# RWKV core of a twelve-part model on one core: chunk parity on partition halves, whole 128x128 transposes

## The reference

```python
def step(state, inp):
    r_t, w_t, k_t, v_t, kk_t, a_t = inp
    sa = jnp.einsum('bhvk,bhk->bhv', state, kk_t)
    state = (state * w_t[:, :, None, :]
             - sa[..., None] * (kk_t * a_t)[:, :, None, :]
             + v_t[..., None] * k_t[:, :, None, :])
    return state, jnp.einsum('bhvk,bhk->bhv', state, r_t)
s0 = jnp.zeros((B, N_HEADS, HEAD_DIM, HEAD_DIM), f32)
_, y = lax.scan(step, s0, (tmaj(rh), tmaj(wh), tmaj(kh), tmaj(vh), tmaj(kk), tmaj(ah)))
```

## Time and profile before

| | |
|---|---|
| median of 3 runs | 2310.64 us (2310.57 to 2314.3) |
| span of the profiled execution | 2303.6 us |
| PE, PEld busy | 2176.2 (94%), 2079.3 (90%) us, 23136 instructions each |
| VectorE (DVE), ScalarE (ACT) busy | 1552.0 (67%), 1204.9 (52%) us |
| mean granted TensorE clock | 0.988 |

### The profile page before, as it was taken

One profiled execution on the slowest core, in us unless ns is written; L12 is line 12 of the kernel. 1 busy time (PEld: TensorE's weight loads), 2 busy tenths in 40 slices (PEclk: granted clock), 3 DMA queues, 4 the chain that ended last, 5 costly groups with the idle time before them and its releaser, 6 DMA issues. The chain is left out here.

```text
span 2303.6 us, 55968 instructions
## 1 busy us (share of the span) xinstructions
PE 2176.2 (94%) x23136; PEld 2079.3 (90%) x23136; DVE 1552.0 (67%) x2405; ACT 1204.9 (52%) x2058; POOL 36.1 (2%) x51
## 2 busy tenths in 40 slices
PE   6887899999999999999989888999999999999998
PEld 6777799999999988899988778999998999898998
DVE  7763465566665688665588735655777777876776
ACT  5733454455544456554458435544676444776443
POOL 0000000000000011000000000000100000100000
PEclk9899999999999999999989999999999999999999
DMA  5310355543455433355533103555333554434553
GB/s 204 128 48 4 110 176 181 180 140 120 153 194 183 163 112 124 123 192 191 183 101 123 54 4 111 192 191 182 129 115 133 193 190 155 147 120 147 182 191 110
DMA packets 88436, 327.16 MB, mean 142 GB/s; under 512 B 9808, under 2 KB 9936, under 8 KB 87632
## 3 DMA queue, kind: packets, MB, share of 16 engines
q1 hardware_dynamic: 87984, 322.66, 41.3%
q0 software_dynamic: 288, 2.10, 0.3%
HBM read 323.67 MB, written 1.05 MB: 141 GB/s over the span
## 5 line engine op out<-in xcount | busy, mean ns | idle before, releaser
L2184 PE MATMUL bank<-h_split,w_split 128*128 128x256 f32 x3176 | 912.7, 287 | 14.3 <-DVE h_split L2403 8.6
L2185 PE MATMUL bank<-h_split,w_split 128*128 128x256 f32 x3176 | 898.1, 283 | 0.0
L2186 PE MATMUL bank<-h_split,w_split 128*128 128x256 f32 x3176 | 897.6, 283 | 0.0
L2372 DVE TENSOR_TENSOR w_split<-ring_a,w_split 128x1024 fp32r<-128x1024 f32 x474 | 568.0, 1224 | 196.9 <-ACT w_split L2269 195.4
L2184 PEld LDWEIGHTS bank<-h_split,w_split 128*128 128x128 f32 x3176 | 602.9, 190 | 26.3 <-DVE h_split L2403 11.3
L2185 PEld LDWEIGHTS bank<-h_split,w_split 128*128 128x128 f32 x3176 | 598.6, 188 | 1.4
L2186 PEld LDWEIGHTS bank<-h_split,w_split 128*128 128x128 f32 x3176 | 597.8, 188 | 0.0
L2269 ACT ACTIVATE w_split<-ring_a 128x1024 fp32r<-128x1024 f32 x474 | 483.4, 1049 | 44.1 <-PE bank L664 23.7
L2206 PE MATMUL bank<-act_split,d_split 128*128 128x256 f32 x1008 | 285.4, 283 | 3.8 <-DVE act_last L2464 2.4
L2207 PE MATMUL bank<-act_split,d_split 128*128 128x256 f32 x1008 | 285.2, 283 | 0.0
L2208 PE MATMUL bank<-act_split,d_split 128*128 128x256 f32 x1008 | 285.1, 283 | 0.0
(11 more groups left out here) (302 smaller groups left out, 3256.4 us busy)
## 6 DMA issues: line engine op xcount, KB each, us to landing
ring_a<-wa SPq DMA_DIRECT2D x474, 512.0 KB, 3.7
ring_d<-wd SPq DMA_DIRECT2D x132, 512.0 KB, 4.3
tab_sb<-tab SPq DMA_DIRECT2D x1, 2384.0 KB, 13.2
hT<-na POOLq DMA_DIRECT2D x2, 1024.0 KB, 5.1
xT<-x SPq DMA_DIRECT2D x1, 1024.0 KB, 4.8
out<-xT SPq DMA_DIRECT2D x1, 1024.0 KB, 3.9
vec_sb<-vec SPq DMA_DIRECT2D x1, 288.0 KB, 4.8
tab_sb<-tab SPq DMA_DIRECT2D x1, 65.0 KB, 4.6
```

What stands on the lines that cost most here:

```text
L2184: mm(dst, w[:, 0, ks], x[:, 0, k, :], start=(k == 0), stop=False)
L2185: mm(dst, w[:, 0, ks], x[:, 1, k, :], start=False, stop=False)
L2186: last = mm(dst, w[:, 1, ks], x[:, 0, k, :], start=False, stop=(k == KT - 1))
L2372: v.tensor_tensor(w_split[:, u % 4, 1, :], ring_a[:, u % 4, :], w_split[:, u % 4, 0, :].bitcast(f32), ALU.subtract).then_inc(s["w_lo"], 1)
```

## The change

Chunk parity, not head parity, is now on partition halves of what the levels hold: partitions 0 to 63 are the even chunk of a pair, 64 to 127 the odd one, and the columns of a head pair n are the two heads side by side. So X of a pair and head pair is a 128x128 block, and its transpose is one `nc.tensor.transpose`. XT and Q have heads on the halves.

- `to_tokens` makes eight 128x128 transposes per call. `level_turned` and `turned_zero` make eight in two groups of four, each into a bank of its own (2 and 3).
- The levels use four banks: product and update both 0 and 1, turned blocks 2 and 3. Scores are in pairs of the banks 4 to 7.
- Both banks of the updated inverse are copied by ScalarE (`copy_x`), into every other 64 columns.
- `mask` works on two banks at a time; for the first pair the key columns of scores 0 and 1 are masked before the query columns. `level0t` goes; the first turned matrix of both chunks comes from TensorE.
- `solve` writes two banks, of which ScalarE copies one (`copy_u`) and VectorE the other (`u_other`), 64 partitions each; u lies where Q was, so the waits of `copy_u` for y and state go.
- `parted` is used 8 times a layer. `gain` and the copies of v_first move before the levels on ScalarE, `gated` behind the first pair's levels on VectorE; `bonus_sum` and `score_part` are spread over the levels.

```diff
-        B = [ctx.enter_context(nc.psum_tensor(f"bank{i}", [P, 512], f32)) for i in range(8)]
+        banks = ctx.enter_context(nc.psum_tensor("banks", [P, 8, 512], f32))
+        B = [banks[:, i, :] for i in range(8)]
...
             def to_tokens(i):
-                b0, b1 = eight(B[i % 4][:, :]), eight(B[i % 4 + 1][:, :])
-                for n, h in each_head():
-                    even = mm(b0[h, n, :], block(i % CHN), ident_of(h), start=True, stop=True)
-                    odd = mm(b1[other(h), n, :], block(i % CHN + 1), ident_of(h), start=True, stop=True)
-                even.then_inc(s["tok_mm"], 1)
-                odd.then_inc(s["tok_mm"], 1)
+                t = slice(P * (i % 4 // 2), P * (i % 4 // 2) + P)
+                for n in range(KT):
+                    block = (qkv[:, 16 + n, t], qkv[:, 8 + n, t], oT[:, n, t])[i // 4]
+                    last = nc.tensor.transpose(B[i % 4 + n // 4][:, P * (n % 4):P * (n % 4) + P], block, T("ident"))
+                    if n % 4 == 3:
+                        last.then_inc(s["tok_mm"], 1)
...
+            def turn_blocks(a, g):
+                for n in range(4 * g, 4 * g + 4):
+                    last = nc.tensor.transpose(turned_bank(g)[:, P * (n % 4):P * (n % 4) + P],
+                                               X_[a // 2][:, P * n:P * n + P], T("ident"))
+                last.then_inc(s[f"xt_mm{g}"], 1)
...
-            def level_turned(a, lv):
-                for n, h in each_head():
-                    even = mm(b0[h, n, :], Xc[a][h, n, :], ident_of(h), start=True, stop=True)
-                    odd = mm(b1[other(h), n, :], Xc[a + 1][h, n, :], ident_of(h), start=True, stop=True)
+            def level_turned(a, lv, g):
+                q = 2 * r + a // 2
+                pe.wait_ge(s["xn_ready"], 8 * q + 2 * lv)
+                pe.wait_ge(s[f"xtn_ready{g}"], 6 * q + lv)
+                turn_blocks(a, g)
...
             def level_product(a, lv):
+                for n, e, t, h, half in blocks():
+                    last = mm(level_bank(t)[h, n, :], scb[a // 2][half, e, n, CH:2 * CH], X_of(a // 2, half, n, e),
+                              start=True, stop=True)
...
             def level_update(a, lv):
+                for n, e, t, h, half in blocks():
+                    last = mm(level_bank(e)[half, n, :], XT_of(a // 2, h, n, t), Q_of(a // 2, h, n, t),
+                              start=True, stop=True)
...
                 if c and second:
-                    if c % 2:
-                        parted(c if c == 1 else 4)
+                    parted((1, 4, 7)[c - 1])
...
-            for i in range(4):
-                score_part(0, i)
-            level_zero(0)
-            level_zero(1)
+            score_part(0, 0)
+            score_part(0, 1)
+            level_zero(0, 0)
+            level_zero(0, 1)
+            score_part(0, 2)
             level_product(0, 1)
-            bonus_sum(0)
-            turned_zero(1)
-            bonus_sum(1)
+            turned_zero(0, 0)
+            turned_zero(0, 1)
+            score_part(0, 3)
...
-            def copy_x(c, lv):
-                q, t = 2 * r + c // 2, c % 2
-                act.wait_ge(s[f"xn_mm{t}"], 4 * q + lv)
-                A(Xc[c], eight(level_bank(c, 1)[:, :]), ACT.Copy).then_inc(s[f"xn_ready{t}"], 1)
+            def copy_x(a, lv):
+                act.wait_ge(s["xn_mm"], 4 * (2 * r + a // 2) + lv)
+                for e in range(2):
+                    A(X_half(a, e), level_bank(e), ACT.Copy).then_inc(s["xn_ready"], 1)
...
             def copy_u(c):
                 act.wait_ge(s["u_mm"], 4 * r + c + 1)
-                if c:
-                    act.wait_ge(s["y_mm"], 5 * r + c)
-                    act.wait_ge(s["st_mm"], 3 * r + c)
-                A(u_, eight(chain_bank(c, "r")[:, :]), ACT.Copy, scale=-1.0).then_inc(s["u_ready"], 1)
+                A(u_[c // 2][half_of(c), 0, :, :], u_banks()[half_of(c), 0, :, :], ACT.Copy, scale=-1.0)\
+                    .then_inc(s["u_ready"], 1)
...
+            def u_other(c):
+                dve.wait_ge(s["u_mm"], 4 * r + c + 1)
+                v.tensor_scalar(u_[c // 2][half_of(c), 1, :, :], u_banks()[half_of(c), 1, :, :], -1.0, None, ALU.mult)\
+                    .then_inc(s["u_side"], 1)
```

More of the change, by code:

```diff
@@ L494, in turned_zero @@
[L494 to L519, removed]
@@ L521, in level_update @@
-            def level_update(a, lv):
[L523 to L533, removed]
-                    even = mm(b0[h, n, :], XTc[a][h, n, :], Qc[a][h, n, :], start=True, stop=True)
-                    odd = mm(b1[h, n, :], XTc[a + 1][o, n, :], Qc[a + 1][o, n, :], start=True, stop=True)
-                even.then_inc(s["xn_mm0"], 1)
-                odd.then_inc(s["xn_mm1"], 1)
@@ L551, in last_turned @@
-            def last_turned(c):
-                q, t = counts(c)
-                pe.wait_ge(s[f"q_ready{t}"], 6 * q + 6)
-                pe.wait_ge(s[f"xtn_ready{t}"], (5 + t) * q + 4 + t)
-                b = eight(level_bank(c, 2)[:, :])
-                for n, h in each_head():
-                    last = mm(b[h, n, :], Qc[c][h, n, :], XTc[c][h, n, :], start=True, stop=True)
-                last.then_inc(s[f"xt_mm{t}"], 1)
+                if a and i == 3:
+                    pe.wait_ge(s["bonus_ready"], 4 * r + 4)
+                elif a or i > 1:
+                    pe.wait_ge(s["score_ready"], 10 * r + (5, 7, 8)[i] if a else 10 * r + i + 1)
@@ new lines, in score_part @@
+                b = score_banks(a, i)
+                for m in range(4 * (i % 2), 4 * (i % 2) + 4):
+                    for e in range(2):
+                        h = slice(HD * e, HD * e + HD)
+                        for c in (a, a + 1):
+                            left = qkv[h, 8 + m, tok(c)] if i >= 2 else oT[h, m, tok(c)]
+                            last = mm(b[half_of(c), e, m % 4, :], left, qkv[h, m:m + 25:24, tok(c)],
+                                      start=True, stop=True)
+                last.then_inc(s["score_mm"], 1)
@@ new lines, in blocks, with level_zero @@
+            def blocks(first=0, count=KT):
+                for n in range(first, first + count):
+                    for e in range(2):
+                        for t in range(2):
+                            yield n, e, t, slice(HD * e, HD * e + HD), slice(HD * t, HD * t + HD)
+            def level_zero(a, e):
+                pe.wait_ge(s["lt_ready"], 4 * r + a + e + 1)
+                if a:
+                    pe.wait_ge(s["q_ready"], 12 * (2 * r + 1))
+                for n in range(KT):
+                    for half in (slice(0, HD), slice(HD, P)):
+                        last = mm(level_bank(e)[half, n, :], scb[a // 2][half, e, n, CH:2 * CH], ident_of(half),
+                                  start=True, stop=True)
+                last.then_inc(s["lz_mm"], 1)
@@ new lines, in unit_lower, with factor_zero @@
+            def unit_lower(a, e):
+                dve.wait_ge(s["score_ready"], 10 * r + (8 if a else 2))
+                lt = scb[a // 2][:, e, :, CH:2 * CH]
+                v.tensor_tensor(lt, lt, wide("eye", KT), ALU.add).then_inc(s["lt_ready"], 1)
+            def factor_zero(a):
+                for e in range(2):
+                    dve.wait_ge(s["lz_mm"], 4 * r + a + e + 1)
+                    v.tensor_tensor(X_half(a, e), level_bank(e), wide("level0", KT), ALU.mult)                        .then_inc(s["q_ready"], 1)
@@ new lines, in factor @@
+            def factor(a, lv):
+                dve.wait_ge(s["lx_mm"], 5 * (2 * r + a // 2) + lv)
+                for t in range(2):
+                    v.tensor_tensor(eight(stream(Q_[a // 2], t)), level_bank(t), wide(f"level{lv}", KT), ALU.mult)                        .then_inc(s["q_ready"], 1)
+            def u_other(c):
+                dve.wait_ge(s["u_mm"], 4 * r + c + 1)
+                v.tensor_scalar(u_[c // 2][half_of(c), 1, :, :], u_banks()[half_of(c), 1, :, :], -1.0, None, ALU.mult)\
+                    .then_inc(s["u_side"], 1)
```

392 lines of the change are left out of this document (205 added, 187 removed).

## The result

| | before | after |
|---|---|---|
| median of 4 runs each | 2310.61 us (2309.42 to 2314.3) | 2270.72 us (2269.39 to 2273.41) |
| span of the profiled execution | 2303.6 us | 2268.4 us |
| PE, PEld busy | 2176.2, 2079.3 us, 23136 instructions each | 2167.8, 2071.8 us, 21472 each |
| clock | 0.988 | 0.990 |

The ratio is 0.9827, interval 0.9812 to 0.9842: 39.9 us less, where 27.6 was forecast; 2283.0 was predicted, and the result lies inside the range of 2261 to 2305, on its low side. 1,664 records went, as counted, but TensorE's busy time fell by only 8.4 us: what went is idle time between records.

The account below looks back on a forecast made before the run. No engine was saturated; round trips and TensorE's stops for instructions filled the two RWKV cores' gaps. Terms -3.5 - 6.2 - 12.5 - 9 + 1.2 + 2.4 = -27.6 us gave span 2276, median 2283; range 2261 to 2305.

Parts of the forecast that it names:

- A: Token transposes at the start of each RWKV core: shorter by 2.1 and 1.4 us in the two layers, -3.5.
- B: First score to first level update: key halves masked first, update at t+10.0 against 12.88 and 13.33, -6.2 us.
- C: Four levels of the first chunk pair: 5.7 us a level including 0.3 for stops, 22.8 a layer, -12.5.
- D: Second pair's levels woven with the state chain: gaps of 9 to 10 halved, 43 us a layer, -9.
- E, waits and switches: Chain's tail to first output unit, plus costs: self-waits +1.2 us, switches between 64x64 and 128x128 shapes +2.4.
- the supply rival: Both cores: instruction supply is the whole bound, 4.3 us per packet, -56 us, 2255; chance of more than -38: 0.12.
- Latency only: Both cores: stops stay at other places, or VectorE's mask holds the levels; about -8 us, 2303; chance 0.2.
- The clock falls: Clock falls in the token transposes and stays low through the first pair's levels; +20 us, 2331; chance 0.1.

Follow-up runs that it names:

- The second run: Changed kernel with v, kb and bb turned to tokens again by 64x64 f32 matmuls instead of whole transposes; 2279.78 us, ratio 0.9874.
- both edits: Changed kernel with both X and the tokens turned again by 64x64 f32 matmuls, all 1,664 records back; 2305.58 us, ratio 0.9990.
- the dummies: Changed kernel plus one-column 64x64 matmuls behind each level update: 16 or 32 in the first pair, 16 in the second; 2275.86, 2287.23, 2277.50 us.
- the wide matmul: Changed kernel with old state carried into new by one 128x512 f32 matmul instead of 16 of 64x64; 2275.38 us, with split inverse copy 2274.45.
- the burst: Changed kernel plus 640 one-column dummy matmuls behind the first level update of a layer; 2407.46 us, ratio 1.0434.

## Why the prediction was right, and where it was off

**A**, forecast -3.5, measured -4.0, with stage A at 7.2 for 7.5. The sum's order of events held. The second run confirms that the stops were the cost: the 64x64 form puts A at 10.0.

**B**, forecast -6.2, measured -7.4, stages 9.42 for 10.0. I gave all of it to the masks' order, and most of it does come with the new order: B had no stop for issue before, and with the turning's records back it still gains 6.6. With the tokens' records back as well it gains 4.1. Of the 3.2 that go, 0.8 is the 64x64 turning by itself and 1.0 a stop in the scores at 158.91; the rest was not separated from a clock of 0.88 in that stage of layer 1.

**C**, forecast -12.5, measured -13.2; a level 5.37 for 5.4, without the 0.3 for stops. The working added up product, turning and copies as if the path had set the 6.37 of before. For levels without a stop that holds (6.38 at 160.36, 5.74 with the old turning in the new layout). But the stops of C were 6.6 us before and none now, and with the turning's records back C is 28.51 and 26.67. So half of the gain is stops, which the working took as gone without a reason. That was close, and luck in part: a level issues 172 records, not 150, and at the usual 3.9 per 127 they need 5.3 of its 5.37. Layer 1's 5.2 more in C, at a clock of 0.89, are in the gain too; the clock need not be their cause, since with both edits C sums to 58.2 at 1.00, for 58.1 before.

**D**, forecast -9, measured -13.4. This is the step that failed in size: "Gaps of 9 to 10 remain; with a fifth of the records gone I halve them: 43". The gaps nearly vanished, 1.6 and 1.0 of idle PE. The windows of before had said how much was to be had: 7.5 and 6.3 of idle PE, of which 12.4 together were stops. Now stops are 0.9, and busy PE is 2.2 less. The trace of before also had the better price: stops in D end 3.98 and 3.88 apart, at 199.31, 203.29 and 207.17:

```profile
199.31 0.21 PE L517 MATMUL bank<-planes 64*64 64x64 f32 x1 [0.32 <-issue]
...
203.29 0.51 PE L641 MATMUL bank<-work,hT 64*64 64x64 f32 x10 [0.51 <-issue]
...
207.17 0.21 PE L515 MATMUL bank<-planes 64*64 64x64 f32 x1 [0.54 <-issue]
```

1,565 records at 3.9 per 127 are 48.1, the stage as measured (layer 2: 47.6 for 46.81). I took 3.40 instead, the shortest of all intervals, and so saw supply as a set of stops on top of a path, where in D it was the pace. At 3.9 the 1,304 records left need 40.0; the stage took 41.0 and 40.5. That is also all but TensorE's own busy time, 39.4. No stop for issue is left in D of layer 2, and 0.9 in layer 1, so by the trace D now stands on TensorE's own work; whether slow delivery also stretches busy stretches is open: the dummies could not tell, and the wide matmul brought a wait of its own.

**E, waits and switches**, forecast +3.6 in all, not located; measured +2.4, all in E. A wait of a solve for the turned copy, 0.8 in each layer and none before, is 1.6 of it; the rest was not traced further. The 1.2 for self-waits is of the right size (0.20 each, four of one line are 0.8; the line of the earlier trace rows is the state part of y, not of the right side); switches between shapes are nowhere visible as a cost: the eight transposes follow the last 64x64 record of the product at once.

**The span and the median.** I set the median 7.0 above the profiled span. All runs listed with a span lie 2.0 to 2.1 above it; the profiled execution of before was simply 4.9 below the median. So 12.3 us of error are 7.6 of the sum (35.2 for 27.6) and 4.7 of this. The 39.9 lie outside the band of the forecast itself (-15 to -38) and in that of the supply rival, which had a chance of 0.12; the result is inside the range only because the range took in part of that rival. By the spans, 35.2, the forecast's band holds.

**The rivals.** *Supply is the whole bound* gave 2255 from 4.3 us a packet and all 13.1 packets gone. Its mechanism is nearer to the truth than I allowed: with the records back 37.6 of 39.9 are gone. But it is not the whole: of the 35.2 between the spans 20.8 are stops, and the 7.4 of B had none. Its price was too high, because 4.3 is the mean over cores in which B and E wait for other things; measured with all that the 64x64 form brings, a packet is worth 2.9 (37.6 / 13.1), 3.7 in the turning (28.9 for 992 records, 7.8 packets), 2.1 in the tokens (10.9 for 5.3). *Latency only* is refuted: by it the stops would have stayed at other places, but of 22.5 us 1.7 are left. *The clock falls* is refuted for this kernel: A to D kept 1.00, stage A with transposes alone included. The Trainium skill (TensorE: Matmul & The Clock Gate, "Part 4: PE-mode transpose") says that transposes do not count as busy for the clock in the way matmuls do; by that rule A was where it would fall, and this trace does not bear it out. Before, and in the kernels with the records back, the clock fell in one or two stages (C 0.89 and 0.94, B 0.88). It was 0.97 in E of layer 2 even in the changed kernel, and 0.91 in E of layer 1 in the kernel with the tokens' records back.

## What to carry to other kernels

Count instructions, not array time, where small f32 matmuls stand in a row: each 64x64 one is two records and two weight loads, and where TensorE stopped for them, the ends of stops in a row were mostly 3.4 to 4.0 us apart. Divide a stage's records by 127 and its time by that; where the result is near what D took with its stops (3.7 to 3.9) and "issue" ends the stops, supply is the pace, and wider instructions help even if the array's work is the same. The quotient alone does not tell: D of the changed kernel has 3.9 to 4.0 with hardly a stop. The packets' own times do: see whether one has landed just before each stop ends. Take the usual interval between the stops' ends, not the shortest, and before adding idle-looking filler, price its own weight loads.

## What the runs showed of the hardware

- TensorE's granted clock was 0.50 (the 1.2 GHz level) from 157 to 224 in the burst, though the profile had it 100% busy for nearly all of it (98 one-column records in 5.00 us). It had been 1.00 through the level's groups of 64 columns and the first dummies (from 153.8), and was 1.00 again from 225, with groups of 64 columns.
- TensorE's stops in rows of 64x64 f32 matmuls end 1.2 to 1.6 us after an instruction packet of 16,384 bytes has landed: all 29 before, all 28 and 32 in the kernels with the turning's and with both parts' records back. The next packet started 1.0 us or more behind the end of a stop.
- A one-column 64x64 f32 record with its weight load, alternating between two quadrants, takes 34 ns at full clock, against 29 for 64 columns on two quadrants and 14.6 over four.
- The self-wait for a 128x512 f32 matmul costs 0.88, that for a group of 64x64 ones 0.20.
- The same instructions, moved by 120 against the program's start, took 1.2 and 2.7 us more in a stage, with waits for issue in place of none. That the blocks' limits fall elsewhere is my reading; the stops in it are waits for packets, but no run moved the limits alone.
